# Router logits by column strips, and a new order of the work around the router on four engines

## The reference

```python
hx = _rmsnorm(x, norm_ffn[i]) * (1 + sc2) + sh2
scores = sigmoid(h @ router_w)                       # (1024, 16)
biased = (scores + router_bias).reshape(n, 4, 4)
best = argmax(top_k(biased, 2).sum(-1))              # the best group of 4 experts
_, idx = top_k(masked to that group, 2)              # its two best experts
w = scores[idx] / sum(scores[idx])
y = sum over e of w_e * ((silu(h @ w_gate[e]) * (h @ w_up[e])) @ w_down[e])
x = x + g2 * y
```

## Time and profile before

| | us |
|---|---|
| median of 3 runs | 1154.33 (1153.88 to 1155.62) |
| the profiled execution, its own time | 1153.68 |
| its span, first to last instruction | 1151.9 |
| PE busy in the span | 1078.0 (94%) |
| DVE busy | 801.8 (70%) |
| ACT busy | 480.8 (42%) |
| POOL busy | 180.1 (16%) |

### The profile page before, as it was taken

How to read it: one execution, slowest core, us unless ns; L and a number is a source line. 1 busy time by engine, 2 the same in 40 slices (tenths; PEclk the granted TensorE clock), 3 DMA queues, 4 the chain that set the end, 5 groups by cost and what they waited for, 6 DMA issues and landing times.

```text
span 1151.9 us, 14883 instructions
## 1 busy us (share of the span) xinstructions
PE 1078.0 (94%) x4739; PEld 792.1 (69%) x4739; DVE 801.8 (70%) x966; ACT 480.8 (42%) x662; POOL 180.1 (16%) x135
## 2 busy tenths in 40 slices
PE   4999999899999999579999999999999999999993
PEld 2554456577777776268888888878887677777772
DVE  5886996788988987356345445444574788888892
ACT  5211224277766775431111111132232366676670
POOL 2101111122222233200000000000000123234232
PEclk9989999999999999899999999999999899999997
DMA  9878649577989973703733233313133888998742
GB/s 367 315 272 315 256 190 416 227 251 206 318 251 314 345 230 79 244 20 126 274 110 109 74 109 127 121 42 148 73 128 151 337 284 261 328 352 280 246 114 47
DMA packets 82002, 243.48 MB, mean 211 GB/s; under 512 B 10016, under 2 KB 34808, under 8 KB 72700
## 3 DMA queue, kind: packets, MB, share of 16 engines
q1 hardware_dynamic: 62436, 188.88, 43.4%
q0 software_dynamic: 17920, 48.31, 16.3%
q10 hardware_dynamic: 1560, 5.26, 1.2%
HBM read 218.29 MB, written 40.89 MB: 225 GB/s over the span
## 4 chain that ended last, share of the span: by engine, by line
PE 68%; DMA 13%; DVE 11%; issue 5%; ACT 2%; SPq 0%; DVEq 0%; POOL 0%; POOLq 0%; ACTq 0%
PE PS L1943 17%; PE PS L1821 8%; PE PS L2046 7%; PE PS L2050 7%; PE PS L2047 7%; DMA out_dram<-YO,TOKI 7%; PE PS L1956 5%; PE PS L1962 4%; DVE ACC L1132 3%; PE PS L1933 3%; PE PS L1672 3%; PE PS L1634 2%; DMA WAE<-in_w_ada_dram 2%; PE PS L1836 1%; DMA x_dram<-YO,TOKI 1%
## 5 line engine op out<-in xcount | busy, mean ns | idle before, releaser
L1453 DVE TENSOR_TENSOR WL<-RAW,WH 128x1024 fp32r<-128x1024 f32 x192 | 225.7, 1219 | 0.2
L926 ACT ACTIVATE WH<-RAW 128x1024 fp32r x184 | 184.6, 1052 | 36.2 <-issue 27.7
L2046 PE MATMUL PS<-HTH,WINH 128*128 128x512 f32 x384 | 150.3, 392 | 5.6 <-DVE HTL L1553 5.3
L1943 PE MATMUL PS<-WH,XTH 128*128 128x512 f32 x368 | 147.2, 400 | 6.3 <-issue 6.2
L2047 PE MATMUL PS<-HTL,WINH 128*128 128x512 f32 x384 | 149.5, 389 | 0.0
L1943 PE MATMUL PS<-WH,XTL 128*128 128x512 f32 x368 | 144.1, 392 | 0.0
L1943 PE MATMUL PS<-WL,XTH 128*128 128x512 f32 x368 | 143.5, 390 | 0.0
L2050 PE MATMUL PS<-HTH,WINL 128*128 128x512 f32 x384 | 118.3, 389 | 0.0
L1956 PE MATMUL PS<-WDR,HETF 128*128 x184 | 88.6, 604 | 4.9 <-DVE YO L1467 4.6
L1467 DVE SCALAR_TENSOR_TENSOR YO<-PS,WOF,ROWS 128x1024 f32<-128x1024 f32 x46 | 59.0, 1284 | 44.2 <-PE PS L1962 31.9
L2046 PEld LDWEIGHTS PS<-HTH,WINH 128*128 128x128 f32 x384 | 72.1, 188 | 22.2 <-DVE HTL L1553 4.8
(11 more groups left out here) (244 smaller groups left out, 1765.4 us busy)
## 6 DMA issues: line engine op xcount, KB each, us to landing
RAW<-in_moe_w_gate_dram SPq DMA_DIRECT2D x32, 1024.0 KB, 7.0
RAW<-in_moe_w_up_dram SPq DMA_DIRECT2D x32, 1024.0 KB, 11.0
WDR<-in_moe_w_down_dram SPq DMA_DIRECT2D x32, 1024.0 KB, 10.0
WA<-in_w_ada_dram SPq DMA_DIRECT2D x28, 1024.0 KB, 7.8
WAE<-in_w_ada_dram SPq DMA_DIRECT2D x12, 1024.0 KB, 9.4
WINR<-in_conv_w_in_dram SPq DMA_DIRECT2D x24, 512.0 KB, 3.8
SLAB<-in_w_ada_dram SPq DMA_DIRECT2D x8, 1024.0 KB, 10.7
X<-x_dram SPq DMA_DIRECT2D x16, 512.0 KB, 5.1
```

Source lines behind the costliest of these rows:

```text
L926: nc.scalar.activation(piece_of(WH[par], i), raw_piece(at, i), ACT.Copy).then_inc(w_high, 1)
L1453: V.tensor_tensor(piece_of(WL[par], i), raw_piece(e, i), piece_of(WH[par], i).bitcast(f32), ALU.subtract).then_inc(w_low, 1)
L1943: ins = T.matmul(bank(2), x[:, ch, :], w[par][:, :, ch, :], start=ch == 0 and i == 0, stop=ch == NC - 1 and i == 2)
L2046: T.matmul(bank(b), WINH[par][:, ch, :], HTH[:, ch, cols], start=ch == 0, stop=False)
```

## The change

The logits of a tile are now made transposed and in strips: the router's weights of one channel block (padded with zeros to 32 columns) are the stationary operand, the tile's 128 tokens the moving one, and the 8 blocks go to four column strips of the array, so that each strip holds the sum of two blocks. ACT copies the 128x128 result (`logits_out`), and one matmul with a constant matrix (C_SUM) adds the four strips and turns the result back (`router`).

Around it the orders are new. In layer 0 `pair(3)` comes before `hidden(4)` and `hidden(5)`; the slabs 2 to 5 are spread between the tiles, and slabs 6 and 7 come behind the table of tokens. In layer 1 the experts of the first six tiles are chosen before `branch_added(7)`, `conv_out(7)` is cut in three, with tile 5's strips and the routers of tiles 4 and 5 between, and ACT loads the tables for Sqrt and Sigmoid explicitly. Small constants moved in memory, two start-up semaphores were merged, and the loads of the router's weights wait for a POOL memset of RW. SP's order in layer 0 has no other edit.

```diff
                 hidden(2)
                 hidden(3)
                 rstd(NORMS0[1])
+                pair(3)
                 hidden(4)
                 hidden(5)
-                pair(3)
                 rstd(NORMS0[2])
                 hidden(6)
                 hidden(7)
+                route_tokens(0)
...
                 rstd(NORMS[2])
                 hidden(6)
+                route_tokens(0)
                 branch_added(7)
                 rstd(NORMS[3])
                 hidden(7)
...
-            route_tokens(0)
             route_tokens(1)
...
             dve.wait_ge(routed, layer + 1)
+            if layer == 0:
+                dve.wait_ge(slab_used, NC)
             weights_low(0, 0, place_of(layer, 0))
...
         sp.dma_start(RB[:], router_bias.partition_broadcast(P)).then_inc(small_in, 16)
-        sp.dma_start(RW[:], router_w.rearrange("(p k) e -> p k e", p=P)).then_inc(small_in, 16)
+        sp.wait_ge(strips_clear, 1)
+        sp.dma_start(RW[:, :, 0:EXPERTS], router_w.rearrange("(p k) e -> p k e", p=P)).then_inc(small_in, 16)
...
+            def logits_out(m):
+                act.wait_ge(logits_mm, layer * NT + m + 1)
+                if m >= 2:
+                    act.wait_ge(router_mm, layer * NT + m - 1)
+                nc.scalar.activation(SUMMAND[m % 2][:], strip_logits(), ACT.Copy).then_inc(logits_ready, 1)
...
+            def table_of(function, step):
+                act.wait_ge(act_begun, step)
+                nc.scalar.activation(WARM[:], WARM[:], function).then_inc(act_begun, 1)
...
                 row_evac_act(4, G2, 6)
-                for m in range(1, 3):
+                for m in range(1, 4):
                     transposed(m)
+                    logits_out(m - 1)
                 square_of(6)
                 square_of(7)
+                transposed(4)
+                logits_out(3)
                 root(NORMS0[2])
-                for m in range(3, 7):
-                    transposed(m)
+                transposed(5)
+                logits_out(4)
+                logits_out(5)
                 sigmoids(0)
-                transposed(7)
+                transposed(6)
+                round_constants()
             else:
...
                 for m in range(3, 6):
                     transposed(m)
+                    logits_out(m - 1)
+                logits_out(5)
+                sigmoids(0)
+                table_of(ACT.Sqrt, 4)
+                round_constants()
                 square_of(7)
                 root(NORMS[3])
+                table_of(ACT.Sigmoid, 5)
                 transposed(6)
-                sigmoids(0)
-                transposed(7)
+            logits_out(6)
+            transposed(7)
+            logits_out(7)
             sigmoids(1)
...
-            def router(m):
+            def strips(m):
                 pe.wait_ge(small_in, 32)
                 pe.wait_ge(hT_ready, n0 + m + 1)
                 if m == 0 and layer == 0:
                     pe.wait_ge(row_evac, 4)
-                b = 6 if m < ROUTED[1][0] else 7
-                at = (m if b == 6 else m - ROUTED[1][0]) * COPIES * EXPERTS
+                if m:
+                    pe.wait_ge(logits_ready, n0 + m)
                 for ch in range(NC):
-                    ins = T.matmul(bank(b)[:, at:at + COPIES * EXPERTS], HTM[m % 2][:, ch, :],
-                                   RW[:, ch, None, :].to_broadcast([P, COPIES, EXPERTS]),
-                                   start=ch == 0, stop=ch == NC - 1)
-                ins.then_inc(router_mm, 1)
+                    strip = slice(ch % 4 * STRIP, (ch % 4 + 1) * STRIP)
+                    ins = T.matmul(strip_logits()[strip, :], RW[:, ch, :], HTM[m % 2][:, ch, :],
+                                   start=ch < 4, stop=ch >= 4, tile_position=(0, ch % 4 * STRIP))
+                ins.then_inc(logits_mm, 1)
+
+            def router(m):
+                pe.wait_ge(logits_ready, n0 + m + 1)
+                b = 6 if m < ROUTED[1][0] else 0
+                at = (m if b == 6 else m - ROUTED[1][0]) * EXPERTS
+                T.matmul(bank(b)[:, at:at + EXPERTS], SUMMAND[m % 2][:], K[:, C_SUM:C_SUM + EXPERTS],
+                         start=True, stop=True).then_inc(router_mm, 1)
...
+            for m in range(3 if layer == 0 else 5):
                 hidden_transposed(m + 1)
+                strips(m)
+                if m:
+                    router(m - 1)
+            if layer == 0:
+                mixer_slab(0)
+                mixer_slab(1)
+                strips(3)
+                router(2)
+                hidden_transposed(4)
+                strips(4)
+                router(3)
+                hidden_transposed(5)
+                mixer_slab(2)
+                strips(5)
+                router(4)
+                mixer_slab(3)
                 router(5)
                 hidden_transposed(6)
+                strips(6)
+                mixer_slab(4)
+                hidden_transposed(7)
+                router(6)
+                mixer_slab(5)
+                strips(7)
+                keep_running(1, 3)
+                router(7)
+            else:
+                conv_out(NT - 1, range(0, 2))
+                strips(5)
+                router(4)
+                conv_out(NT - 1, range(2, 4))
+                router(5)
+                conv_out(NT - 1, range(4, NC))
+                hidden_transposed(6)
+                keep_running(5)
+                strips(6)
+                hidden_transposed(7)
+                router(6)
                 keep_running(1)
+                strips(7)
                 keep_running(1)
+                router(7)
...
                      start=True, stop=True)
-            if layer == 0:
-                mixer_slab(6)
-                mixer_slab(7)
             keep_running(3 if layer else 2, spare)
...
             ins.then_inc(table_mm, 1)
-            keep_running(1, 4)
+            if layer == 0:
+                mixer_slab(6)
+                mixer_slab(7)
+            else:
+                keep_running(1, 4)
```

More of the change, by code:

```diff
@@ L276, in backbone @@
     WHI, WLO = r.put("WHI", [P, TOP * NT], f32r), r.put("WLO", [P, TOP * NT], f32r)
-    TINY = r.put("TINY", [P, 24, 40])
+    TINY = r.put("TINY", [P, 18, 40])
+    SUMMAND = [r.put(f"SUMMAND{i}", [P, P]) for i in range(2)]
     assert r.at <= base + width(arena.shape) - 32, (r.at - base, width(arena.shape))
@@ L849, in sigmoids, with round_constants @@
                         act.wait_ge(pair_read, 4)
-                    nc.scalar.activation(LOWR[:], lower, ACT.Copy)
-                    nc.scalar.activation(ONER[:], ones, ACT.Copy).then_inc(rounded, 1)
-                logits = bank(6 + i)[:, 0:(last - first) * COPIES * EXPERTS].rearrange("p (m k e) -> p m k e", k=COPIES, e=EXPERTS)
-                nc.scalar.activation(SMALL[:, 0, first:last], logits[:, :, 0], ACT.Sigmoid).then_inc(scores_ready, 1)
+                act.wait_ge(router_mm, layer * NT + last)
+                logits = bank(6 - 6 * i)[:, 0:(last - first) * EXPERTS].rearrange("p (m e) -> p m e", e=EXPERTS)
+                nc.scalar.activation(SMALL[:, 0, first:last], logits, ACT.Sigmoid).then_inc(scores_ready, 1)
+            def round_constants():
+                nc.scalar.activation(LOWR[:], lower, ACT.Copy)
+                nc.scalar.activation(ONER[:], ones, ACT.Copy).then_inc(rounded, 1)
+            def table_of(function, step):
+                act.wait_ge(act_begun, step)
+                nc.scalar.activation(WARM[:], WARM[:], function).then_inc(act_begun, 1)
             if layer == 0:
@@ L891, in _ @@
                 transposed(1)
+                logits_out(0)
                 transposed(2)
+                logits_out(1)
                 root(NORMS[2])
@@ L995, in _ @@
                 high(1, 1, 1, None)
-                act.wait_ge(warm, 2)
-                nc.scalar.activation(WARM[:], WARM[:], ACT.Sqrt).then_inc(warm, 1)
+                act.wait_ge(act_begun, 3)
+                nc.scalar.activation(WARM[:], WARM[:], ACT.Sqrt).then_inc(act_begun, 1)
                 for tiles in NORMS_BACK:
@@ L1357, in route_tokens @@
                 V.tensor_tensor(BOTH[:, m0:m1], t3(7), t3(8), ALU.add).then_inc(mask_ready, 1)
-            route_tokens(0)
+            if layer == 0:
+                pair(0)
+                for b in range(ADA_MIXER + 12, N_ADA):
+                    ada_first(b)
+                pair(1)
+                dve.wait_ge(row_evac, 2)
+                scale_row(0, 3, 6)
+                rstd(NORMS0[0])
+                dve.wait_ge(row_evac, 3)
+                hidden(0)
+                hidden(1)
+                pair(2)
+                hidden(2)
+                hidden(3)
+                rstd(NORMS0[1])
+                pair(3)
+                hidden(4)
+                hidden(5)
+                rstd(NORMS0[2])
+                hidden(6)
+                hidden(7)
+                route_tokens(0)
+            else:
+                for m in range(4):
```

(22 more changed lines are left out.)

128 lines of the change are left out of this document (34 added, 94 removed).

## The result

The changed kernel takes 1168.58 us (median of 4 executions, 1163.94 to 1175.45) against 1154.11 of the kernel before in the same comparison: 1.0131 times as long [1.0106, 1.0155]. I had forecast 1159.4. The direction and the trigger are as forecast, the size is not: +14.5 us instead of +5.1, outside my range. The execution profiled took 1169.78 us, span 1167.9, at a mean granted clock of 0.966 (before 1153.68, 1151.9, 0.980).

The account below looks back on a forecast made before the run. The chain was taken as 68% PE and 11% DVE, movable only where each router stage hands over to its experts. Layer 0 +3.9 and layer 1 +1.2 gave +5.1, 1159.4 us; own range 1156.3 to 1163.7, 8 in 10 1152.8 to 1164.

Parts of the forecast that it names:

- the trigger: Layer 0: hidden(4) written 7.75 us later, so SP issues RAW at 175.75 and PE waits at mixer_slab(2).
- layer 1's "+1.2": Layer 1's stage: route_tokens(1) starts at 889.75 in place of 888.60, +1.15, between +0.7 and +3.4.
- the table's term of layer 0, "-2.3": Layer 0, route_tokens(1) to TOKI: 13.8 us instead of 16.07 with slabs 6 and 7 gone, -2.3.
- cover of slabs and weights' table: Layer 0 after TOKI: slabs and weights' table lie beside the gather and DVE's last steps, free; without cover 1.6 us.
- the sigmoid's table: Layer 1, ACT: the Sigmoid table is loaded ahead of its wait, as in the first slot; scores come at 872.15.
- By then the clock should be back: Layer 0, PE: after five pieces at the slow price, full clock from route_tokens(0)'s end at 200.3; route_tokens(1) at 202.25.
- +3.9 forecast: Layer 0's whole stage: route_tokens(1) +6.2 and the table -2.3 give +3.9, between +1.3 and +6.0.
- The slab wait: Layer 0, PE at mixer_slab(2): waits 9.5 us for slabs 2 and 3, slab 3 landing at 189.1.
- The strips: Router on PE: sixteen records with 32 stationary columns take 0.45 us a tile, with 0.23 and 0.47 as ends.
- The switch of table: Layer 1, ACT: loading the Sigmoid table between root and tile 6's copy costs 1.3 us, not the skill's 2.66.
- The clock rival: The clock stays down in both stages: layer 0 +6.0, layer 1 +3.4, 1163.7; chance 0.15.
- the main case: The forecast itself: late slab stream in layer 0, +5.1 us in all, own range +2.0 to +9.4; chance 0.55.

Follow-up runs that it names:

- pair3_back: The changed kernel with VectorE's pair(3) back behind hidden(5) in layer 0, SyncE's order untouched; 1159.46 us, ratio 1.0041 to the kernel before.
- before_pair3: The kernel before with only VectorE's pair(3) moved ahead of hidden(4) and hidden(5) in layer 0; 1158.37 us, ratio 1.0041.
- loads_first: The changed kernel with expert 0's weights and slabs 2 to 5 issued on SyncE ahead of the store of H 4; 1154.35 us, ratio 0.9996.
- slabs_last: layer1_old with slabs 2 to 5 on TensorE behind router(7) in layer 0; 1155.82 us, ratio 1.0024 to the kernel before.
- warm: The changed kernel with 12 filler matmuls on TensorE ahead of mixer_slab(2) in layer 0; 1170.22 us, ratio 1.0145 to the kernel before.
- slabs67_front: The changed kernel with slabs 6 and 7 back ahead of the tokens' table; 1168.56 us, ratio 1.0116 to the kernel before.
- table_early: loads_first with the Sigmoid table loaded ahead of logits_out(5) in both layers; 1157.69 us, ratio 1.003; run again 1152.64 us, 1.0003.
- gap_filled: best67 with 6 instead of 3 filler matmuls on TensorE ahead of layer 0's count; 1149.28 us, ratio 0.9964 to the kernel before.
- best: loads_first with layer 1's order as before, strips kept; 1150.97 us, ratio 0.9976 to the kernel before.
- best67: best with slabs 6 and 7 back ahead of the tokens' table; 1151.05 us, ratio 0.9978 to the kernel before.
- combined: gap_filled with slabs 2 to 5 on TensorE behind router(7) in layer 0; 1151.48 us, ratio 0.9981 to the kernel before.
- before_loads: The kernel before with RAW and slabs 2 to 5 issued on SyncE ahead of the store of H tiles 4 and 5; 1151.46 us, ratio 0.9983.
- warm_old1: layer1_old with 12 filler matmuls on TensorE ahead of mixer_slab(2) in layer 0; 1170.52 us, ratio 1.0135 to the kernel before.
- layer1_old: The changed kernel with layer 1's order on three engines as before, strips kept; 1162.55 us, ratio 1.0068 to the kernel before.

## Why the prediction was wrong in size

**Right.** hidden(4) late, the SyncE order behind it, the wait on TensorE at mixer_slab(2), and the router's tiles behind that: the trigger was found from the order of the queue and the landing times, and pair3_back, before_pair3, loads_first and slabs_last show it. RAW's issue was forecast for 175.75 and came at 174.66.

**The steps that failed** are two terms of the sum: layer 1's "+1.2", and the table's term of layer 0, "-2.3", with the cover of slabs and weights' table taken as free (0 us, "else 1.6"). The first was mis-sized at any clock, the second holds only at the full one, and each of the two profiles of the changed kernel has a long stretch at 1.2 GHz in one of the two stages.

*Layer 1.* For +1.2 the two profiles have +2.5 and +7.0, and giving back the old order takes 6.0 us off the median. Up to route_tokens(1) it is +4.1 in both where I had +1.15, for the reasons under the sigmoid's table below. In the first profile 1.5 of these came back at the table, whose clock was 1.00 there. In the second they did not (route_tokens(1) to TOKI 15.23 us, as before), and from TOKI to the first transposes it was 8.5 us instead of 5.7, mostly at 1.2 GHz (0.50 in 915 to 920 us).

*Layer 0's table.* After route_tokens(1) TOKI took 16.18 us in the first profile, 2.4 more than forecast, as PE's table matmuls ran at 1.2 GHz (1.89 and 2.51 us). From TOKI to the first transposes it was 10.46 us instead of 5.60 before (217.71 after the earlier trace rows's TOKI): slabs, weights' table and fillers end at 231.5, and no cover was left. That is 4.9 us where I had 0. In the second profile the two are 13.69 (my 13.8) and 7.0 us, at a granted clock of 0.76 over the second. At 1.00 both parts of the term held: loads_first and warm, with the same order there, have 13.7 us and then 5.7 and 5.6. So the step that failed is the price, the full clock for everything behind route_tokens(1) ("By then the clock should be back"). slabs67_front, with the slabs ahead of the table again, has the same median as the changed kernel: of the -2.3 nothing shows in the time.

For layer 0 as a whole, +3.9 forecast, the profiles have +13.3 and +5.5. In the second, RAW's issue is 5.5 us later than before (173.46 against 167.99), and from there to gate_up it is 54.3 us, as before: layer 0 lost just what the stream was late.

**The slab wait**, 9.5 us forecast, 12.07 measured. I had counted 5.0 MB at 375 GB/s between RAW's issue and slab 3, 13.3 us; the window shows 17.03 us at 386 GB/s, 6.6 MB. I had taken 1.05 MB of stores of x out of the stream of before. But in 168 to 184.1 there GpSimd's queue, which has the stores of x and of the odd tiles of H, moved only 0.52 MB, and in the new window it moved 1.46. Slabs 4 and 5 land 19.5 and 23.0 us after RAW's issue, 19.4 and 23.1 before: the stream came later and was no shorter. RAW itself was issued 1.1 us ahead of my forecast, which leaves +2.6.

**The sigmoid's table.** I took it to be loaded ahead of the wait. It was loaded behind it in both layers: 196.42 and 886.81, released by PE. In layer 0 tile 6's copy stood behind it on ScalarE, and of the 8.78 us of route_tokens(1) (6.2 forecast) this and the slab are the excess; the clock was back earlier than I took it, which gave some back. In the second profile it is 7.5 us. In layer 1 the scores came at 888.10; branch_added(7) was late by 3.5 us, counted from the transposes of H 0 (2.1 forecast). After it TensorE idled 3.01 us, and tile 7's transposes were paid at 1.2 GHz (1.95 us, my bound's "double"). In table_early the load is ahead of the wait, and 2.7 us of the 4.1 come back in the profile.

**The strips.** 0.64 us for 16 records (first to last end), with a step of 0.57, where I had 0.45 and 0.47 as the upper end; at 1.2 GHz 1.08. On a dozen strips at full clock this is 1.4 us or so (12 x 0.12), an estimate, and most of it lies inside waits.

**The switch of table** cost 1.3 us: WARM ends at 899.46, 1.49 us after the load of 897.97 began. Against the 2.66 us of the Trainium skill ("ScalarE: Activation LUTs", What ACT_TABLE_LOAD costs) these rows side with my choice.

**The clock rival** was half right. It had a chance of 0.15 and the low clock in both stages; each of the two profiles has the long stretch at 1.2 GHz in one of them only. Neither it nor the main case had room for a stall of 12 us and a table at 1.2 GHz in one sum.

## What to carry to other kernels

Before one operation is moved ahead of another, look at the stores that hang on the second, and at every load behind those in the issuing queue: here 6.7 us on VectorE were some 9 us at the end (pair3_back), and two lines on SyncE gave back 14, since they put the stream ahead of where it had been before. Don't put a matmul that waits for a transfer ahead of work that is ready unless the rows show the transfer to be early; slabs_last shows the price, 6.7 us. And work called covered has to be covered at 1.2 GHz as well, or the term is not zero.

And one profile of a stage whose clock varies can put a loss in the wrong place: the first had most of it in layer 0, the second in layer 1, and only the runs without one part each told what a part costs.

The version to keep is gap_filled: the strips, layer 1's old order, loads ahead of the store, fillers before the count, 0.36% [0.22, 0.5] under the kernel before. Its lead over best, best67, combined and before_loads lies within the intervals.

## What was unexpected of the hardware

The same layer 0 code came out very unlike in two profiles: from RAW's first issue to gate_up(0) 53.7 us in loads_first and 62.1 in best, with TensorE at 0.50 from 205 to 220 us in the second. A stretch at 1.2 GHz lasts 3 to 5 us in some places and some 20 in others. Windows of best:
```profile
205.00:215.00 10.00, 9.93 (x40) 5.88 (x40) 6.44 (x17) 0.60 (x1) 2.06 (x2) 0.50 0.61 229
```
TensorE is 99% busy there, so that idling at the moment is no reason for it. A single profile of such a stage is therefore uncertain by some 8 us; the medians are what the verdicts rest on. Why warm_old1 is 8 us slower than layer1_old in all five executions (1168.22 and up, against 1159.39 to 1165.44) stays open; its profile shows the slab 1.5 us later behind RAW's issue, and some 20 us at 0.50.
